# Keys and squares of an mLSTM head shared out anew between ScalarE and VectorE

## The chip, the cores and the metric

The program runs on one core of a Trainium2 chip. The metric is device time in microseconds for one execution, the median of several. The engines are called here as in the profile: PE is TensorE (PEld its weight loads), DVE is VectorE, ACT is ScalarE, POOL is GpSimd, SP is SyncE.

## The reference, cut to what matters

The reference is a transformer block followed by a second one, for 1024 positions and 1024 features, all in fp32. The change touches only the mLSTM of the first block: 4 heads of dimension 128, each run forward and backward in time, the two results added, normalised by their root mean square and gated:

```python
def step(carry, chunk):
    C, n, m = carry
    qc, kc, vc, ic, fc = chunk
    ...
    a = g[..., None] - b + ic
    m_new = jnp.maximum(g + m, jnp.max(a, axis=-1))
    decay = jnp.exp(g + m - m_new)
    w = jnp.exp(a - m_new[..., None])
    C = decay[..., None, None] * C + jnp.einsum('bhs,bhsv,bhsd->bhvd', w, vc, kc)
    n = decay[..., None] * n + jnp.einsum('bhs,bhsd->bhd', w, kc)
    return (C, n, m_new), h
...
h = (h_fw + h_bw).transpose(0, 2, 1, 3)
h = h * lax.rsqrt(jnp.mean(h * h, axis=-1, keepdims=True) + EPS)
h = h * norm_g.astype(jnp.float32).reshape(MLSTM_HEADS, MLSTM_HEAD_DIM)
h = h.reshape(B, S, MLSTM_WIDTH) * jax.nn.sigmoid(o_pre.astype(jnp.float32))
```

The keys weighted by `w` are needed once for each direction, since `w` differs. The mean of the squares is taken over the 128 numbers of a head, for each of the 1024 positions.

## The kernel before

All orders are fixed when the program is built. A plan (`schedule`) lists steps such as `("mk", h, u)`; each engine walks the same list and issues its own part of each step, in order, and counting semaphores tie the engines together. So an instruction that waits holds up everything behind it on its engine.

A head's 1024 positions lie as 8 chunks of 128. For the mLSTM the steps are, with `h` the head, `d` the direction and `u` a half of the positions:

- `mk` (PE `m_keys` L1072, DVE `m_keys` L1864): PE transposes 4 chunks of keys into one PSUM bank. DVE reads the bank twice, multiplies by the key coefficients of direction 0 and then of direction 1 and writes `kp[h % 2][0]` and `kp[h % 2][1]` (the rows call both `m_kp`, 128x512 each). Semaphore `k_made` counts both.
- `mv` (ACT `m_values` L1450): the transposed values are copied by ACT to `m_v`.
- `mm` (ACT L1466): ACT makes four exponentials of 128x128 for the decay weights `m_w`. `ms`, `wt`: scores by PE, product by DVE.
- `mu` (PE L1116, DVE `m_states` L1889): PE makes the chunk updates from `m_v` and `m_kp`; DVE runs them through a chain of 7 states `m_cs` (L1897 and L1901).
- `mo` (PE L1133, L1136): the outputs of a head and direction, in banks 5 to 7, in three parts.
- `mf`, `mi`, `mg`: the denominator `m_den`. ACT takes absolute values and a logarithm (L1474, L1475, L1477), DVE the maximum (`m_largest` L1904), ACT the exponential (L1482); then ACT (L1492, direction 0) or DVE (L1915, direction 1) scales the eight chunks into `m_hs`.
- `mq`, `mr`, `mn`: the normalisation. ACT squares all of `m_hs` in one instruction (L1499), DVE adds up the squares of each position (`m_sums`, L1920), ACT makes the inverse roots (L1503, L1505), DVE scales `m_hs` (`m_norm` L1922).
- `mtr` (PE L1143, DVE L1930): `m_hs` is turned back and gated.

The functions that transpose into or multiply into PSUM banks take them from a ring (`M_BANK`): two banks while the attention of the block still runs, five afterwards. `ring_emptied` (L865) gives what must be over before PE may write a bank again; for a bank that held keys this is that `kp` has been made from it.

Head 0 is prepared in the middle of the attention's last two heads, between its score and value steps. After the attention, `memory` (L235) writes out head `h` while it prepares head `h + 1`. In its order, shortened, an iteration is: `mo(h,0)` with `mk(h+1)` and `mv(h+1)` between its parts, `mf(h,0)`, `mm(h+1,0,0)`, `mi`, `mg`, `mu(h,1)`, `mm(h+1,0,1)`, `mtr(h-1)`, `mu(h+1,0)`, `mm(h+1,1)`, `ms`, `wt`, `mo(h,1)` with `mw(h+1)`, `mf(h,1)`, `mi`, `mg`, `mq(h)`, `mr(h)`, `mn(h)`. The iteration for head 3 prepares nothing, and the first products of the output projection come behind it.

Of the kernel before, what the change touches and what calls it, by code (L numbers as in the profile page):

```python
# [15 lines left out]
P = 128  # L16
# [49 lines left out]
for _name, _n in (("b_ada", 48), ("b_ada_2", 24), ("norm_mix_g", 8), ("norm_ffn_g", 8),  # L66
# [21 lines left out]
    "sel_in g_act g_vec g_tr g_cols st_hi st_lo sel_made sums_one k_tr k_made v_tr v_made m_mm e_made s_mm wgt wr_mm qp_made "  # L88
    "u_mm state out_mm den_abs den_ln den_max den_inv h_part h_sum o_sq o_sum o_ln o_r o_n o_tr o_done "

# [6 lines left out]
class Plan:  # L97
# [12 lines left out]
    def no(self, kind, *which):  # L110
        return self.number[(kind, *which)]
# [422 lines left out]
def tile_of(k):  # L534
    return slice(k * P, (k + 1) * P)


def build(nc, a, out):
# [3 lines left out]
    with ExitStack() as ctx:  # L542
# [322 lines left out]
        def ring_emptied(step):  # L865

            same = [x for x in M_RING[:M_RING.index(step)] if M_BANK[x] == M_BANK[step]]
            if not same:
                return None
            x = same[-1]  # L870
            if x[0] == "mk":
                return s["k_made"], 2 * no(*x)
            if x[0] == "mu":
                return s["state"], state_no(*x[1:])
            if x[0] == "ms":
                return s["wgt"], no("wt", x[1], 1, x[2])
            return s[{"mv": "v_made", "mm": "e_made", "mw": "qp_made", "mtr": "o_done"}[x[0]]], no(*x)
# [30 lines left out]
        def tensor(e):  # L908
# [158 lines left out]
            def ring(step):  # L1067
                if emptied := ring_emptied(step):
                    e.wait_ge(*emptied)
                return M_BANK[step]  # L1070

# [37 lines left out]
            def m_states(h, d, g):  # L1109
                bank = ring(("mu", h, d, g))  # L1110
                e.wait_ge(s["k_made"], 2 * no("mk", h, 1))
                e.wait_ge(s["v_made"], no("mv", h, 1))
                e.wait_ge(s["sums_one"], 1 + h % 2)
                for i, c in enumerate(M_GROUPS[g][:1 if g == 2 else 3]):
                    j = chunk(d, c)
                    x = e.matmul(ps[:, bank, m_piece(g, i)], kp[h % 2][d][:, j, :], v1[h % 2][:, j, :], start=True, stop=True, skip_group_check=True)  # L1116
                x.then_inc(s["u_mm"], 1)
# [145 lines left out]
        def scalar(e):  # L1263
# [150 lines left out]
            def gate(part):  # L1414
# [31 lines left out]
                elif part == 18:  # L1446
                    e.wait_ge(s["g_tr"], 4)
                    copy(dec_cols[:, :, :].rearrange("p a b -> p (a b)"), ps[:, aux_bank("gate", 18), 0:64]).then_inc(s["g_cols"], 1)

            def m_values(h, u):  # L1450
                e.wait_ge(s["v_tr"], no("mv", h, u))
                if h >= 2:
                    e.wait_ge(s["out_mm"], outs_no(2 * (h - 1)))
                copy(v1[h % 2][:, 4 * u:4 * u + 4, 0:P], ps[:, M_BANK[("mv", h, u)], :].rearrange("p (a b) -> p a b", a=4)).then_inc(s["v_made"], 1)
# [40 lines left out]
            def m_squares(h):  # L1495
                e.wait_ge(s["h_sum"], KT * (h + 1))
                if h:
                    e.wait_ge(s["o_sum"], h)
                e.activation(sq_m[:, :, :], hs[h % 2][:, :, :], ACT.Square).then_inc(s["o_sq"], 1)  # L1499

# [137 lines left out]
            def y_norm(n):  # L1638
# [3 lines left out]
                    "rsq": head_squares, "rln": head_roots, "attend": attend, "khi": k_high, "qhi": q_high, "mrow": mrow, "sc": scores, "take": take,  # L1642
                    "gate": gate, "mv": m_values, "mm": m_decays, "mf": m_finish, "mi": m_inverse, "mg": m_divide, "mq": m_squares,
                    "mr": m_roots, "mixk": mix, "wout": wout, "nr": norm, "nt": normed,
# [8 lines left out]
        def vector(e):  # L1653
            def tt(dst, x, z, op):
                return e.tensor_tensor(dst, x, z, op)  # L1655
# [208 lines left out]
            def m_keys(h, u):  # L1864
                e.wait_ge(s["k_tr"], no("mk", h, u))
                if h >= 2:
                    e.wait_ge(s["u_mm"], 6 * (h - 1))
                elif h == 1:
                    e.wait_ge(s["div"], 16)
                for d in range(2):  # L1870
                    x = kc_cols[:, 4 * u:4 * u + 4, d, h:h + 1].to_broadcast([P, 4, P])
                    tt(kp[h % 2][d][:, 4 * u:4 * u + 4, :], ps[:, M_BANK[("mk", h, u)], :].rearrange("p (a b) -> p a b", a=4), x,
                       ALU.mult).then_inc(s["k_made"], 1)

# [33 lines left out]
            def m_divide(h, d):  # L1908
                if d:
                    e.wait_ge(s["den_inv"], m_no(h, d) + 1)  # L1910
                    for c in range(KT):
                        j = chunk(1, c)
                        if c == 0:
                            e.wait_ge(s["h_part"], KT * (h + 1))
                        e.scalar_tensor_tensor(hs[h % 2][:, j, :], ps[:, 5 + c // 3, m_piece(c // 3, c % 3)][:, 0:P], den[1][:, c:c + 1],  # L1915
                                               hs[h % 2][:, j, :], ALU.mult, ALU.add).then_inc(s["h_sum"], 1)

            def m_sums(h):
                e.wait_ge(s["o_sq"], h + 1)
                e.tensor_reduce(o_sum[:, :], sq_m[:, :, :], AX_X, ALU.add).then_inc(s["o_sum"], 1)  # L1920

# [171 lines left out]
            def y_tile(n, k):  # L2093
# [9 lines left out]
                    "max": max_unit, "mrow": mrow, "div": divide, "gate": gate,  # L2103
                    "mk": m_keys, "wt": m_weights, "mw": m_queries, "mu": m_states, "mf": m_largest, "mg": m_divide, "mq": m_sums,
                    "mn": m_norm, "mtr": m_turn, "mixk": mix, "acc1": first_sums, "wout": wout, "nt": normed, "nl": normed_last, "fs": second_sum, "ft": final_normed,
# [310 lines left out]
```

## Time and profile before

| | us |
|---|---|
| median of 3 runs | 2150.54 (2149.56 to 2150.75) |
| the profiled execution, its own time | 2150.5 |
| its span in the profile | 2148.7 |
| PE busy in the span | 2043.8 (95%) |
| DVE, ACT busy | 1109.3, 871.1 |

The span is measured from the first to the last recorded instruction; what lies around it makes up the other 1.8 us. The mLSTM's steps lie between 491 and 650 us from the start of the span. In a row of the timeline there stand: start in us, length in us, engine, line, operation, what it writes and reads, how many instructions were merged, and in brackets how long the engine had been idle before and what ended the idle time. The length of a merged row reaches from the first start to the last end; the next instruction on ACT or DVE often starts a tenth of a microsecond before the end of the one ahead.

### The profile page before, as it was taken

The page shows a single profiled execution, that of the slowest core. Times are in us where ns is not written, and L with a number is a line of the kernel's source. Part 1 is how long each engine was busy: PE and PEld are TensorE (multiplying, and loading weights), DVE is VectorE, ACT ScalarE, POOL GpSimd, SP SyncE. Part 2 cuts the span into 40 slices and gives each one's busy share as a digit, 9 for nine tenths or more (in the row PEclk, how much of TensorE's full clock was granted, in tenths as well). Part 3 has the DMA queues.
Part 4 walks back from the last instruction along what each step waited for, and adds up shares of the span by engine and source line. Part 5 has one row for each costly group of instructions (what it writes and reads, how often), then busy time and mean ns, then how long its engine had stood idle before and what let it go on. Part 6 is the DMA issues. An engine that isn't in the chain of part 4 may idle for free.

```text
span 2148.7 us, 23710 instructions
## 1 busy us (share of the span) xinstructions
PE 2043.8 (95%) x9232; PEld 1590.5 (74%) x9232; DVE 1109.3 (52%) x1534; ACT 871.1 (41%) x1315; POOL 61.5 (3%) x115
## 2 busy tenths in 40 slices
PE   4999999999889899999999999999999999999797
PEld 1778876656777788888888888887787876776485
DVE  5785747555665655533354333437343454435535
ACT  4433345555443433233243232324424664445542
POOL 1001000000000000000000000000010000000000
PEclk9999999999999999999999999999999999999898
DMA  8335410000204546523333223334331010003043
GB/s 334 98 120 195 162 33 10 18 32 1 89 1 147 185 150 193 182 95 126 122 104 133 94 97 103 128 122 147 98 120 48 30 40 30 20 21 128 0 167 118
DMA packets 63198, 217.12 MB, mean 101 GB/s; under 512 B 6640, under 2 KB 7792, under 8 KB 62832
## 3 DMA queue, kind: packets, MB, share of 16 engines
q1 hardware_dynamic: 48944, 161.07, 22.2%
q0 software_dynamic: 14144, 54.53, 7.4%
q8 instruction: 75, 1.23, 0.2%
q14 instruction: 35, 0.29, 0.0%
HBM read 187.79 MB, written 25.17 MB: 99 GB/s over the span
## 4 chain that ended last, share of the span: by engine, by line
PE 84%; DVE 6%; ACT 4%; DMA 2%; issue 2%; SPq 1%; POOL 0%; DVEq 0%; ACTq 0%
PE ps L911 21%; PE ps L913 20%; PE ps L912 20%; PE ps L1045 8%; PE ps L1021 2%; PE ps L1022 2%; PE ps L988 2%; DMA w_raw<-in_weights 2%; PE ps L1003 1%; DMA cmask<-in_consts 1%; DVE slot L1655 1%; SPq L2206 1%; DVE w_lo L1659 1%; ACT w_hi L1265 1%; PE ps L991 1%
## 5 line engine op out<-in xcount | busy, mean ns | idle before, releaser
L911 PE MATMUL ps<-h_hi,w_hi 128*128 128x512 f32 x1504 | 600.0, 399 | 22.6 <-DVE h_lo L1692 11.0
L913 PE MATMUL ps<-h_hi,w_lo 128*128 128x512 f32 x1504 | 589.7, 392 | 0.0
L912 PE MATMUL ps<-h_lo,w_hi 128*128 128x512 f32 x1504 | 589.1, 392 | 0.0
L1659 DVE TENSOR_TENSOR w_lo<-w_raw,w_hi 128x1024 fp32r<-128x1024 f32 x222 | 271.8, 1225 | 496.5 <-ACT w_hi L1265 495.0
L1265 ACT ACTIVATE w_hi<-w_raw 128x1024 fp32r<-128x1024 f32 x222 | 234.7, 1057 | 527.2 <-DMA w_raw<-in_weights 525.5
L911 PEld LDWEIGHTS ps<-h_hi,w_hi 128*128 128x128 f32 x1504 | 285.2, 190 | 87.7 <-issue 21.7
L913 PEld LDWEIGHTS ps<-h_hi,w_lo 128*128 128x128 f32 x1504 | 284.2, 189 | 60.6
L912 PEld LDWEIGHTS ps<-h_lo,w_hi 128*128 128x128 f32 x1504 | 284.9, 189 | 59.0 <-issue 1.9
L1783 DVE TENSOR_REDUCE mh<-ps 128x1 f32<-128x512 f32 x192 | 124.8, 654 | 149.8 <-PE ps L988 70.7
L911 PE MATMUL ps<-hid_hi,w_hi 128*128 128x512 f32 x352 | 136.9, 389 | 0.0
L912 PE MATMUL ps<-hid_lo,w_hi 128*128 128x512 f32 x352 | 136.9, 389 | 0.0
L913 PE MATMUL ps<-hid_hi,w_lo 128*128 128x512 f32 x352 | 136.9, 389 | 0.0
L1045 PE MATMUL ps<-full_pf,full_v 128*128 128x512 f32 x256 | 132.0, 598 | 0.3 <-ACT full_pf L1402 0.2
L1045 PE MATMUL ps<-second_pf,second_v 128*128 128x128 f32 (+3 forms) x336 | 115.9, 447 | 7.5 <-ACT second_pf L1402 7.2
L1402 ACT ACTIVATE full_pf<-ps 128x512 f32<-128x512 f32 x128 | 76.2, 596 | 99.5 <-PE ps L1022 99.0
L911 PE MATMUL ps<-mix_hi,w_hi 128*128 128x512 f32 x256 | 103.2, 403 | 6.9 <-DVE mix_lo L1659 6.9
L912 PE MATMUL ps<-mix_lo,w_hi 128*128 128x512 f32 x256 | 101.5, 397 | 0.0
L913 PE MATMUL ps<-mix_hi,w_lo 128*128 128x512 f32 x256 | 101.2, 395 | 0.0
L1402 ACT ACTIVATE second_pf<-ps,cum_cols 128x512 f32<-128x512 f32 (+1 forms) x96 | 55.4, 579 | 111.3 <-PE ps L1026 75.4
L1021 PE MATMUL ps<-full_qq,full_kk 128*128 128x512 f32 x128 | 91.0, 711 | 0.1
L1021 PE MATMUL ps<-second_qq,second_kk 128*128 128x128 f32 (+3 forms) x168 | 85.3, 508 | 0.3 <-issue 0.3
L911 PEld LDWEIGHTS ps<-hid_hi,w_hi 128*128 128x128 f32 x352 | 66.1, 188 | 13.8
(302 smaller groups left out, 2593.5 us busy)
## 6 DMA issues: line engine op xcount, KB each, us to landing
w_raw<-in_weights SPq DMA_DIRECT2D x222, 512.0 KB, 3.5
ada_next<-in_ada POOLq DMA_DIRECT2D x32, 512.0 KB, 4.7
ada_last<-in_ada POOLq DMA_DIRECT2D x24, 512.0 KB, 4.3
ada_first<-in_ada SPq DMA_DIRECT2D x8, 1024.0 KB, 14.9
m_scratch<-y POOLq DMA_DIRECT2D x12, 512.0 KB, 4.8
xt<-in_x SPq DMA_DIRECT2D x2, 2048.0 KB, 16.9
y<-m_scratch SPq DMA_DIRECT2D x4, 1024.0 KB, 5.9
x_again<-in_x SPq DMA_DIRECT2D x16, 256.0 KB, 3.7
```

The source lines that it names most:

```text
L911: e.matmul(o, w_hi[slot][:, tile_of(kw)], hi, start=start, stop=False)
L912: e.matmul(o, w_hi[slot][:, tile_of(kw)], lo, start=False, stop=False)
L913: return e.matmul(o, w_lo[slot][:, tile_of(kw)], hi, start=False, stop=stop)
L988: x = e.matmul(ps[:, bank, 0:k1 - k0], q(qt), A.kk[kb][:, k0:k1], start=True, stop=(kind == "full"), skip_group_check=True)
L991: x = e.matmul(ps[:, bank, 0:k1 - k0], sel_f[:, h, :], cum_split[:, k0:k1], start=False, stop=not diagonal, skip_group_check=True)
L1021: e.matmul(o, A.kk[kb][:, keys], A.qq[b][:, q], start=True, stop=False, skip_group_check=True)
L1022: x = e.matmul(o, A.ka[kb][0:65, keys], A.qa[b][0:65, q], start=False, stop=not masked, skip_group_check=True)
L1045: x = e.matmul(o, A.v[kb][:, kt, :], A.pf[p3][:, c:c + q1 - q0], start=(u == 0 and kind != "band"), stop=False, skip_group_check=True)
L1265: return e.activation(dst, src, ACT.Copy)
L1402: e.activation(A.pf[p3][:, c0:c1], ps[:, bank, c0:c1], ACT.Exp, scale=SC, **bias).then_inc(s["p_exp"], 1)
L1659: return e.tensor_tensor(dst, src, hi.bitcast(F32), ALU.subtract)
L1783: x = e.tensor_reduce(to, ps[:, bank, 0:k1 - k0], AX_X, ALU.max)
```

## The change

Three things change, all in the mLSTM.

The squares: instead of one ACT instruction of 128x1024 and a DVE reduction, ACT issues eight instructions of 128x128, each of which also writes the sum of its squares to a column of `o_sum` (an accumulator output). They wait, as before, for all eight chunks of `m_hs`. The step `m_sums` of DVE and the semaphore `o_sq` are gone.

The keys: DVE makes only the keys of direction 0. Those of direction 1 are made by ACT, with four instructions of 128x128 for each half, which wait until DVE's have been made (`k_made`), and count `k_late`. In ACT's order they stand where `mk` stands in the plan, ahead of the copies of the values `mv`.

The waits of PE: a bank that held keys is free when both `k_made` and `k_late` have come; the updates `mu` wait for the one of their direction.

```diff
     def ring_emptied(step):
             if x[0] == "mk":
-                return s["k_made"], 2 * no(*x)
+                return s["k_made"], no(*x)
...
             def ring(step):
                 if emptied := ring_emptied(step):
                     e.wait_ge(*emptied)
+                    if emptied[0] is s["k_made"]:
+                        e.wait_ge(s["k_late"], emptied[1])
...
             def m_states(h, d, g):
                 bank = ring(("mu", h, d, g))
-                e.wait_ge(s["k_made"], 2 * no("mk", h, 1))
+                e.wait_ge(s["k_late" if d else "k_made"], no("mk", h, 1))
...
         def scalar(e):
+            def m_keys(h, u):
+
+                e.wait_ge(s["k_made"], no("mk", h, u))
+                if h >= 2:
+                    e.wait_ge(s["u_mm"], 6 * (h - 1))
+                elif h == 1:
+                    e.wait_ge(s["div"], 16)
+                else:
+                    e.wait_ge(s["g_cols"], 4)
+                for c in range(4):
+                    x = e.activation(kp[h % 2][1][:, 4 * u + c, :], ps[:, M_BANK[("mk", h, u)], tile_of(c)], ACT.Copy,
+                                     scale=kc_cols[:, 4 * u + c, 1, h:h + 1])
+                x.then_inc(s["k_late"], 1)
...
             def m_squares(h):
                 e.wait_ge(s["h_sum"], KT * (h + 1))
                 if h:
-                    e.wait_ge(s["o_sum"], h)
-                e.activation(sq_m[:, :, :], hs[h % 2][:, :, :], ACT.Square).then_inc(s["o_sq"], 1)
+                    e.wait_ge(s["o_r"], h)
+                for c in range(KT):
+                    x = e.activation(sq_m[:, c, :], hs[h % 2][:, c, :], ACT.Square, accum_out=o_sum[:, c:c + 1])
+                x.then_inc(s["o_sum"], 1)
...
         def vector(e):
             def m_keys(h, u):
-                for d in range(2):
-                    x = kc_cols[:, 4 * u:4 * u + 4, d, h:h + 1].to_broadcast([P, 4, P])
-                    tt(kp[h % 2][d][:, 4 * u:4 * u + 4, :], ps[:, M_BANK[("mk", h, u)], :].rearrange("p (a b) -> p a b", a=4), x,
-                       ALU.mult).then_inc(s["k_made"], 1)
+                x = kc_cols[:, 4 * u:4 * u + 4, 0, h:h + 1].to_broadcast([P, 4, P])
+                tt(kp[h % 2][0][:, 4 * u:4 * u + 4, :], ps[:, M_BANK[("mk", h, u)], :].rearrange("p (a b) -> p a b", a=4), x,
+                   ALU.mult).then_inc(s["k_made"], 1)
...
-            def m_sums(h):
-                e.wait_ge(s["o_sq"], h + 1)
-                e.tensor_reduce(o_sum[:, :], sq_m[:, :, :], AX_X, ALU.add).then_inc(s["o_sum"], 1)
```

PE's instructions stand in the same order as before; only their waits differ. The order on ACT and DVE changes as follows.

ACT between the end of head 0 and the denominator of head 1, before (`m_hs_192` is head 0's, `m_v_179` holds the values of head 2, `m_den_185` is the denominator of direction 0):

```order
L1499 ACTIVATE m_sq<-m_hs_192 128x1024
L1503 ACTIVATE o_root<-o_sum,small 128x8
L1505 ACTIVATE o_root<-o_root 128x8
L1265 ACTIVATE m_v_179<-ps 128x4x128 x2
L1474 ACTIVATE m_den_185<-ps 128x6
L1475 ACTIVATE m_den_185<-ps 128x2
L1477 ACTIVATE m_den_185<-m_den_185,small 128x8
```

and the same place now:

```order
L1516 ACTIVATE m_sq,o_sum<-m_hs_192 128x128 x8
L1521 ACTIVATE o_root<-o_sum,small 128x8
L1523 ACTIVATE o_root<-o_root 128x8
L1462 ACTIVATE m_kp_181<-ps,kc_cols 128x128 x8
L1267 ACTIVATE m_v_179<-ps 128x4x128 x2
L1490 ACTIVATE m_den_185<-ps 128x6
L1491 ACTIVATE m_den_185<-ps 128x2
L1493 ACTIVATE m_den_185<-m_den_185,small 128x8
```

Eight scalings of keys stand between the roots and the copies of the values, and the denominator of head 1 comes behind both.

DVE at the same place, before (`m_kp_180` and `m_kp_181` are the keys of head 2 for direction 0 and 1, `m_cs_177` the states of head 1, direction 1):

```order
L1920 TENSOR_REDUCE o_sum<-m_sq 128x8
L1655 TENSOR_TENSOR m_hs_192<-m_hs_192,o_root 128x1024
L1655 TENSOR_TENSOR m_kp_180<-ps,kc_cols 128x512
L1655 TENSOR_TENSOR m_kp_181<-ps,kc_cols 128x512
L1655 TENSOR_TENSOR m_kp_180<-ps,kc_cols 128x512
L1655 TENSOR_TENSOR m_kp_181<-ps,kc_cols 128x512
L1655 TENSOR_TENSOR m_den_185<-m_den_185,n_cols 128x8
L1897 COPY m_cs_177<-ps 128x129
L1901 SCALAR_TENSOR_TENSOR m_cs_177<-m_cs_177,dec_cols,ps 128x129 x6
```

and now:

```order
L1673 TENSOR_TENSOR m_hs_192<-m_hs_192,o_root 128x1024
L1673 TENSOR_TENSOR m_kp_180<-ps,kc_cols 128x512 x2
L1673 TENSOR_TENSOR m_den_185<-m_den_185,n_cols 128x8
L1914 COPY m_cs_177<-ps 128x129
L1918 SCALAR_TENSOR_TENSOR m_cs_177<-m_cs_177,dec_cols,ps 128x129 x6
L1943 SCALAR_TENSOR_TENSOR y<-ps,small,y 128x512 x2
```

Three instructions are gone from DVE's row. The maximum of the denominator (`m_den_185<-m_den_185,n_cols`) still stands ahead of the states, and its input now comes from behind ACT's scalings.

ACT in the attention, where head 0 is prepared, before:

```order
L1402 ACTIVATE full_pf_126<-ps 128x512
L1381 ACTIVATE full_qa_121<-ps 1x512
L1402 ACTIVATE full_pf_127<-ps 128x512
L1265 ACTIVATE full_qq_117<-y 64x512
L1265 ACTIVATE m_v_179<-ps 128x4x128
```

and now:

```order
L1404 ACTIVATE full_pf_126<-ps 128x512
L1383 ACTIVATE full_qa_121<-ps 1x512
L1462 ACTIVATE m_kp_181<-ps,kc_cols 128x128 x4
L1404 ACTIVATE full_pf_127<-ps 128x512
L1267 ACTIVATE full_qq_117<-y 64x512
L1267 ACTIVATE m_v_179<-ps 128x4x128
```

Four scalings stand between two exponentials of the attention (`full_pf`), ahead of the copy of the values; the four for head 0's first half stand in the same way one exponential earlier.

## Rows read from the trace of the kernel before

**Rows 1.** The page, part 1: busy time and share of the span.

```profile
PE 2043.8 (95%) x9232; PEld 1590.5 (74%) x9232; DVE 1109.3 (52%) x1534; ACT 871.1 (41%) x1315; POOL 61.5 (3%) x115
```

**Rows 2.** Windows: stretch, its length, then busy us of each engine, PE clock, DMA.

```profile
484.00:540.00 56.00, 54.38 (x233) 34.63 (x232) 30.58 (x57) 28.92 (x59) 0.00 (x0) 1.00 0.00 1
564.00:585.00 21.00, 19.76 (x152) 18.32 (x152) 17.45 (x38) 10.24 (x36) 0.00 (x0) 0.92 0.00 1
```

**Rows 3.** Groups by form, 544 to 650: busy us, mean ns | idle before.

```profile
L1492 ACT ACTIVATE m_hs<-ps,m_den 128x128 f32<-128x128 f32 x32 | 8.7, 383 | 0.1
L1655 DVE TENSOR_TENSOR m_kp<-ps,kc_cols 128x512 f32<-128x512 f32 x12 | 7.4, 682 | 1.9 <-PE ps L1078 1.9
L1499 ACT ACTIVATE m_sq<-m_hs 128x1024 f32<-128x1024 f32 x4 | 4.2, 1057 | 9.0 <-DVE m_hs L1915 9.0
L1920 DVE TENSOR_REDUCE o_sum<-m_sq 128x8 f32<-128x1024 f32 x4 | 4.9, 1220 | 3.4 <-ACT m_sq L1499 3.4
```

**Rows 4.** Groups by form, 690 to 900: VectorE reading its accumulator.

```profile
L1677 DVE DVE_READ_ACCUMULATOR2_ANT mod<- 128x1 f32 x20 | 1.6, 82 | 0.0
```

**Rows 5.** Timeline where head 0 is prepared, DVE, ACT and PE's weight loads.

```profile
496.19 1.29 DVE L1655 TENSOR_TENSOR m_kp<-ps,kc_cols 128x512 f32<-128x512 f32 x2 [0.60 <-PE ps L1078]
...
496.66 0.60 ACT L1402 ACTIVATE full_pf<-ps 128x512 f32<-128x512 f32 x1 [1.41 <-PE ps L1022]
...
498.19 0.60 ACT L1265 ACTIVATE m_v<-ps 128x512 f32<-128x512 f32 x1 [0.28 <-PE ps L1084]
...
500.58 0.60 ACT L1265 ACTIVATE m_v<-ps 128x512 f32<-128x512 f32 x1
...
501.41 0.78 PEld L1116 LDWEIGHTS ps<-m_v,m_kp 128*128 128x128 f32 x6 [0.53 <-ACT m_v L1265]
```

**Rows 6.** Timeline of head 0's iteration, DVE, ACT and PE.

```profile
547.01 2.48 DVE L1655 TENSOR_TENSOR m_kp<-ps,kc_cols 128x512 f32<-128x512 f32 x4 [1.91 <-PE ps L1078]
...
550.55 0.18 ACT L1474 ACTIVATE m_den<-ps 128x6 f32<-128x6 f32 x1 [0.25 <-PE ps L1136]
...
555.55 0.50 PE L1091 MATMUL ps<-nm_stack,sel 128*128 128x512 f32 x1 [1.94 <-ACT m_w L1466]
```

**Rows 7.** Timeline of head 1's iteration, ACT.

```profile
565.69 1.06 ACT L1499 ACTIVATE m_sq<-m_hs 128x1024 f32<-128x1024 f32 x1 [2.23 <-DVE m_hs L1915]
568.03 0.30 ACT L1503 ACTIVATE o_root<-o_sum,small 128x8 f32<-128x8 f32 x1 [1.29 <-DVE o_sum L1920]
...
570.11 1.09 ACT L1265 ACTIVATE m_v<-ps 128x512 f32<-128x512 f32 x2 [1.54 <-PE ps L1084]
571.44 0.18 ACT L1474 ACTIVATE m_den<-ps 128x6 f32<-128x6 f32 x1 [0.24 <-PE ps L1136]
...
571.71 0.30 ACT L1477 ACTIVATE m_den<-m_den,small 128x8 f32<-128x8 f32 x1
```

**Rows 8.** Timeline of head 1's iteration, DVE.

```profile
568.61 1.23 DVE L1655 TENSOR_TENSOR m_hs<-m_hs,o_root 128x1024 f32<-128x1024 f32 x1 [0.61 <-ACT o_root L1505]
569.75 2.48 DVE L1655 TENSOR_TENSOR m_kp<-ps,kc_cols 128x512 f32<-128x512 f32 x4
572.14 0.16 DVE L1655 TENSOR_TENSOR m_den<-m_den,n_cols 128x8 f32<-128x8 f32 x1
572.64 0.29 DVE L1897 COPY m_cs<-ps 128x129 f32<-128x129 f32 x1 [0.33 <-PE ps L1116]
```

**Rows 9.** Timeline of head 2's iteration, DVE.

```profile
597.07 1.57 DVE L1901 SCALAR_TENSOR_TENSOR m_cs<-m_cs,dec_cols,ps 128x129 f32<-128x129 f32 x4 [0.70 <-PE ps L1116]
598.97 1.41 DVE L1930 SCALAR_TENSOR_TENSOR y<-ps,small,y 128x512 f32<-128x512 f32 x2 [0.33 <-PE ps L1143]
```

**Rows 10.** Timeline of PE: heads 1 and 2 on keys, and head 3's iteration.

```profile
566.73 1.57 PE L1078 MATMUL ps<-ident,y 128*128 128x128 f32 x8
...
587.60 1.04 PE L1078 MATMUL ps<-ident,y 128*128 128x128 f32 x8
...
615.63 0.63 PE L1143 MATMUL ps<-ident,m_hs 128*128 128x128 f32 x4 [0.38 <-DVE m_hs L1655]
```

More of the change, by code:

```diff
@@ L88 @@
     "sel_in g_act g_vec g_tr g_cols st_hi st_lo sel_made sums_one k_tr k_made v_tr v_made m_mm e_made s_mm wgt wr_mm qp_made "
-    "u_mm state out_mm den_abs den_ln den_max den_inv h_part h_sum o_sq o_sum o_ln o_r o_n o_tr o_done "
+    "u_mm state out_mm den_abs den_ln den_max den_inv h_part h_sum k_late o_sum o_ln o_r o_n o_tr o_done "
     "mix_hi mix_lo xa_in0 xa_in1 x1_made x1_kept silu gmul hid_hi hid_lo xc_in0 xc_in1 x2_made xb_kept "
@@ L1642, in scalar @@
                     "rsq": head_squares, "rln": head_roots, "attend": attend, "khi": k_high, "qhi": q_high, "mrow": mrow, "sc": scores, "take": take,
-                    "gate": gate, "mv": m_values, "mm": m_decays, "mf": m_finish, "mi": m_inverse, "mg": m_divide, "mq": m_squares,
+                    "gate": gate, "mk": m_keys, "mv": m_values, "mm": m_decays, "mf": m_finish, "mi": m_inverse, "mg": m_divide, "mq": m_squares,
                     "mr": m_roots, "mixk": mix, "wout": wout, "nr": norm, "nt": normed,
@@ L2103, in vector @@
                     "max": max_unit, "mrow": mrow, "div": divide, "gate": gate,
-                    "mk": m_keys, "wt": m_weights, "mw": m_queries, "mu": m_states, "mf": m_largest, "mg": m_divide, "mq": m_sums,
+                    "mk": m_keys, "wt": m_weights, "mw": m_queries, "mu": m_states, "mf": m_largest, "mg": m_divide,
                     "mn": m_norm, "mtr": m_turn, "mixk": mix, "acc1": first_sums, "wout": wout, "nt": normed, "nl": normed_last, "fs": second_sum, "ft": final_normed,
```

## The prediction

> **What bounds the kernel now.** First the page's busy times: PE is busy for 2043.8 of 2148.7 us, the others about half or less [rows 1]. A microsecond on DVE or ACT is therefore worth something only where PE waits for it, and the change touches nothing outside the mLSTM. Next the windows over that stage. While head 0 is prepared, in the attention, PE is busy for 54.38 of 56 us. In the iteration of head 1 it is busy for 19.76 of 21, and its granted clock there averages 0.92; DVE has 17.45 [rows 2]. Then the timeline, engine by engine. What the reader is to see in it is who waits for whom between one head and the next: ACT squares the head, DVE adds up, ACT makes the roots, DVE scales the head and then the next keys, and runs the states [rows 7, 8]. From 568.61 DVE has hardly a gap, so in head 1 DVE sets the pace. ACT meanwhile copies the values and stands ready early: it begins head 1's denominator at 571.44 [rows 7], and DVE's maximum follows at 572.14 [rows 8].
>
> **The squares.** Before, from the start of the squares to the start of the logarithm is 568.03 - 565.69 = 2.34 us: 1.06 on ACT, 1.22 on DVE and two hand-overs [rows 3, 7]. Now ACT issues eight instructions with an accumulator output. They wait for all eight chunks of the head as before, so nothing starts sooner. No row shows ACT with an accumulator. Call the new time from squares to logarithm X. From below: if cutting up and accumulating cost nothing, X is the 1.1 us of the one instruction [rows 3]. From above: each chunk takes the full 0.38 us of a 128x128 activation with no overlap, and a read of the accumulator as long as the smallest ACT instruction, 0.18 [rows 3, 7]: 8 x 0.56 = 4.5. Nearer rows: eight 128x128 activations one behind the other take 2.17 (0.27 each); with 0.08 for a read, as DVE's own read of its accumulator has it [rows 4], that is 0.35, or 0.46 if the read lets nothing overlap. The middle is 0.40 a chunk, X = 3.2, a loss of 0.86 against 2.34. The 2.17 is the length of the eight scalings by L1492, 32 in all at 383 ns each in 8.7 us busy [rows 3].
>
> On this the Trainium skill, page "ScalarE: Activation LUTs", section "What ACT_TABLE_LOAD costs", states 186 ns plus 0.833 ns per element for an ACTIVATE with immediate operands, and 93 ns of overlap back to back: 200 ns a chunk, 1.7 us for eight by an estimate from that page. The trace agrees for the large form (1057 ns for 1024 elements) and shows nothing of the accumulator. With 1.7 the sum below would be 2.5.
>
> **The keys.** DVE loses one 682 ns multiplication for each half of the keys, 0.62 from start to start (2.48 for four) [rows 3, 8]. ACT gains four scalings for each, the same form as L1492: PSUM in, a column as scale. That is 2.17 for a head's eight. The same page of the Trainium skill, section "Rules for kernel authors", says to use VectorE rather than ScalarE for a multiplication. The rows agree in fp32 too, 682 ns against half of 2.17. Who is slower matters less, though, than where the eight stand: behind DVE's, and ahead of ACT's copies of the values and of the denominator, for whose maximum DVE waits in order ahead of its states. PE's two new waits fall behind these and cost nothing by themselves.
>
> *Head 0, in the attention.* DVE's first multiplication of the second half ends at 496.19 + 0.68 = 496.87. ACT scales from 496.9 and has room for the next instruction at 498.0, so the exponential that stood at 496.66 is 1.34 late. The copy waited 0.28 for PE at 498.19 [rows 5], so 1.06 remains, and ACT is full from there to the last copy at 500.58. PE's update at 501.41 was released by that copy: it comes 1.06 late. PE is the bound here, so 1.1 stays.
>
> *Head 0's iteration* (keys of head 1). ACT used to wait here. Now: DVE's multiplication from 547.01, 0.68 and 0.04 to hand over, eight scalings 2.17, two copies 1.09 [rows 6, 7] gives 550.99 for the denominator that began at 550.55. ACT's chain from there ends in the decay weights for which PE waited at 555.55 [rows 6]. PE is late by 0.4. DVE's gain of 1.24 is hidden: it had nothing to do.
>
> *Head 1's iteration* (keys of head 2), from the squares at 565.69 [rows 7, 8]: X 3.2; logarithm to DVE's scaling of the head 0.58; 1.14 to the keys; 0.68 + 0.04 to ACT; 2.17 of scalings; 1.09 of copies; from the denominator's start to its maximum 572.01 - 571.44 and a hand-over, 0.60. Sum 9.50, so the maximum at 575.2 instead of 572.14, the states at 575.4 instead of 572.64. Here DVE turns from busy to idle, for 4.58 - 1.30 = 3.3 us (0.72 + 2.17 + 1.09 + 0.60, less two multiplications). The states, the turned head and the next states follow in one row, and PE's outputs behind them: 2.7 late.
>
> *Head 2's iteration* is the same sum with one rounding of weights more on both engines. The maximum is 3.0 late; DVE had waited 0.70 and 0.33 for PE behind it [rows 9], which absorb 1.0. So 2.0.
>
> *Head 3's iteration* has no keys. PE waited for the scaled head at 615.63 [rows 10]: late by X - 2.34 = 0.86. The last head's squares lie beside the output projection, which starts without them. With 0.86 more they still do, cost 0.
>
> **Sum.** 1.1 + 0.4 + 2.7 + 2.0 + 0.9 = 7.1 us. The profiled execution took 2150.5 (span 2148.7 and 1.8 around it), the median of the runs shown is 2150.54, so both give 2157.6. X enters three times: 2.2 gives 2154.6, 4.5 gives 2161.5, and 1.1 gives 2151.3.
>
> **Rivals.**
> - *The accumulator is nearly free* (X from 1.1 to 2.2). For it: the two fixed costs seen are small, 0.08 and 0.18. Against: a result that is read out must be complete first. 0.8 to 4.1 late, at 2.0 it is 3.5: 2154.0. By the page's 200 ns a chunk it would be here. Within 0.2%.
> - *PE's clock falls in the new gaps.* The eight transposes of head 1 took 1.57 where head 2's took 1.04 [rows 10], and the granted clock of that window is 0.92, a mix of 2.4 and 1.2 GHz: 0.08 of 21 us [rows 2] is 1.7 us of full clock lost in one spell. In heads 1 and 2 PE now idles for longer, in pieces. Two spells on the path: 3.4 more, 2161.0. Against: after 1.94 us of idle at 555.55 a 128x512 product took 0.50 [rows 6], so not every such gap brings a spell.
> - *The accumulator is dear* (X near 4.5): 2161.5.
> - *DVE's shorter queue decides* and the time falls. The mechanism: DVE is the pace from 568.61 on, and loses 1.24 in heads 1 and 2; if squares cost the bare 1.1, another 1.24 in three places. 2 x 1.24 + 3 x 1.24 = 6.2 less, 2144.3. It decides only if ACT has the logarithm of the denominator ready when DVE has finished its two multiplications, 1.30 after their start. By my sum it is ready 0.72 + 2.17 + 1.09 + 0.60 = 4.58 after it, 3.3 too late whatever X is. Unlikely.
>
> **How the numbers follow.** The forecast as summed, 4.3 to 9 us late, 48%; accumulator free 21%; clock 15%; accumulator dear 10%; DVE decides 6%. 0.2% of the time is 4.3 us, about what a measurement of this kernel can tell from no change. Faster by more than that: the last case, 5%. Within it: the free accumulator and what little the last case leaves, 22%. Slower: 73%. Predicted 2157.6; the range reaches down into the free accumulator and up over clock and dear accumulator: 2152 to 2163.
>
> **What the profile would show.** The squares: eight ACT instructions of 128x128 and the logarithm 3.2 behind the first; below 2.2 or above 4 one of the accumulator's rivals holds. The keys: DVE idle for some 3 us ahead of the head's denominator in heads 1 and 2, with ACT busy on `m_kp` and `m_v`; if DVE goes on without a gap, the main step is wrong. Attention: the update of head 0 waits 1.6 for ACT's copy instead of 0.5. Clock: the granted clock of the windows of heads 1 and 2, by the lengths of equal groups of PE. I would be wrong throughout if the stretch from the first keys to the output projection grew by less than 4 us.

## The result, and the profile after

| | before | after |
|---|---|---|
| median of 12 runs each, us | 2149.59 | 2155.72 |
| lowest, highest | 2146.83, 2152.56 | 2152.10, 2160.15 |
| profiled execution's span | 2148.7 | 2154.1 |

The ratio is 1.0028, with an interval of 1.0019 to 1.0036: 4.1 to 7.7 us slower, 6.1 by the medians. Forecast were 7.1 slower and 2157.6.

The page of the profile after, part 1, against [rows 1]: DVE has lost 9.3 us and 12 instructions, ACT has gained 13.8 and 92, and PE has the same work.

```profile
PE 2043.8 (95%) x9232; PEld 1590.2 (74%) x9232; DVE 1100.0 (51%) x1522; ACT 884.9 (41%) x1407; POOL 61.5 (3%) x115
```

ACT of the profile after, from the squares of head 0 to the logarithm of head 1's denominator:

```profile
565.16 0.31 ACT L1516 ACTIVATE m_sq<-m_hs 128x128 f32<-128x128 f32 x1 [2.22 <-DVE m_hs L1932]
565.38 0.19 ACT L1516 ACTIVATION_READ_ACCUMULATOR m_sq<-m_hs 128x1 f32 x1
565.47 0.29 ACT L1516 ACTIVATE m_sq<-m_hs 128x128 f32<-128x128 f32 x1
...
567.64 0.30 ACT L1521 ACTIVATE o_root<-o_sum,small 128x8 f32<-128x8 f32 x1
567.97 0.21 ACT L1523 ACTIVATE o_root<-o_root 128x8 f32<-128x8 f32 x1
570.08 2.17 ACT L1462 ACTIVATE m_kp<-ps,kc_cols 128x128 f32<-128x128 f32 x8 [1.89 <-DVE m_kp L1673]
572.09 1.13 ACT L1267 ACTIVATE m_v<-ps 128x512 f32<-128x512 f32 x2
573.04 0.25 ACT L1490 ACTIVATE m_den<-ps 128x6 f32<-128x6 f32 x1
```

and DVE of the same stretch:

```profile
568.21 1.23 DVE L1673 TENSOR_TENSOR m_hs<-m_hs,o_root 128x1024 f32<-128x1024 f32 x1 [3.09 <-ACT o_root L1523]
569.36 1.28 DVE L1673 TENSOR_TENSOR m_kp<-ps,kc_cols 128x512 f32<-128x512 f32 x2
573.71 0.17 DVE L1673 TENSOR_TENSOR m_den<-m_den,n_cols 128x8 f32<-128x8 f32 x1 [3.07 <-ACT m_den L1493]
573.80 0.29 DVE L1914 COPY m_cs<-ps 128x129 f32<-128x129 f32 x1
```

Two things are to be seen. The squares hardly cost: from the first of them to the logarithm there are 567.64 - 565.16 = 2.48 us against 2.34. And DVE, which ran without a gap at this place in [rows 8], now stands idle for 3.07 us ahead of the maximum, while ACT first waits for DVE's keys (1.89), then scales, copies and takes the denominator. From the start of the squares to the maximum 8.55 us pass, before 6.45.

### The profile page after: what moved, and what is told of

Its sections match the earlier page's. It is cut to its first block, busy times and chain, and to the rows that moved or that the text cites. A ratio compares the mean times of both kernels' runs of the same rounds, so it can differ in the third digit from the quotient of the medians.

```text
span 2154.1 us, 23801 instructions
## 1 busy us (share of the span) xinstructions
PE 2043.8 (95%) x9232; PEld 1590.2 (74%) x9232; DVE 1100.0 (51%) x1522; ACT 884.9 (41%) x1407; POOL 61.5 (3%) x115
## 4 chain that ended last, share of the span: by engine, by line
PE 83%; DVE 6%; ACT 5%; DMA 3%; issue 2%; SPq 1%; POOL 0%; DVEq 0%; ACTq 0%
PE ps L911 20%; PE ps L913 20%; PE ps L912 20%; PE ps L1045 8%; PE ps L1021 2%; PE ps L1022 2%; PE ps L988 2%; DMA w_raw<-in_weights 2%; PE ps L1003 1%; DMA cmask<-in_consts 1%; SPq L2219 1%; DVE slot L1673 1%; DVE w_lo L1677 1%; ACT w_hi L1267 1%; PE ps L991 1%
## 5 line engine op out<-in xcount | busy, mean ns | idle before, releaser
L1045 PEld LDWEIGHTS ps<-second_pf,second_v 128*128 128x128 f32 x336 | 60.2, 198 | 24.4 <-ACT second_pf L1404 10.7
```

Source lines behind the costliest of these rows:

```text
L1045: x = e.matmul(o, A.v[kb][:, kt, :], A.pf[p3][:, c:c + q1 - q0], start=(u == 0 and kind != "band"), stop=False, skip_group_check=True)
```

## The experiments

The time of a run is the median of 5 to 12 executions, and its ratio is to the kernel before on the same chip. The kernel before had medians of 2148.6 to 2150.8 on the chips used, so two runs are best compared by what each is over it; the changed kernel is 6.1 over it. `e12_before_again` is a single execution.

**Which part of the change costs?** `e1_squares` is the kernel before with the new `m_squares` alone. `e2_keys` is the changed kernel with the old squares and `m_sums`:

```diff
 e1:            keys as before; in m_squares
-                e.activation(sq_m[:, :, :], hs[h % 2][:, :, :], ACT.Square)
+                for c in range(KT):
+                    x = e.activation(sq_m[:, c, :], hs[h % 2][:, c, :], ACT.Square, accum_out=o_sum[:, c:c + 1])
 e2:            keys as changed; this edit taken back, m_sums again on DVE
```

> Only the squares are changed: eight with an accumulator output on ScalarE, VectorE's reduction gone, both directions of the keys on VectorE as before. Theory A (the keys' place in ScalarE's row costs the time): from squares to logarithm 2.48 us in place of 2.34, so 0.14 for each of heads 0, 1 and 2, in all 0.4 us over the kernel before: 2150.0, no measurable difference. Theory B (the split squares cost the time): most of the 6.1 us, 2154 or more. Theory C (half of it arises after the mLSTM stage, whatever the stage does): the piece in the stage is 0.4, the whole is 2 or more.

Measured: 2150.53 against 2150.47, ratio 1.0005 (0.9996 to 1.0013). Split squares cost nothing that can be measured.

> Only the keys are changed: direction 1 on ScalarE behind VectorE's, squares in one instruction with VectorE's reduction as before. Theory A: VectorE idles some 3 us ahead of the maximum in heads 1 and 2 as in the changed kernel, the stage up to the output projection is 3.4 us longer than before (0.4 in the attention, 0.2, 1.7, 1.1), time 2153 to 2155. Theory B: below 2150.6. Theory C: 3.4 in the stage and 2 more behind it, 2155.

Measured: 2155.75, ratio 1.0028 (1.0017 to 1.0038), the changed kernel's own ratio. The whole loss is the keys'. Theory B is refuted.

**Is it where the scalings stand in ACT's row?** `e3_keys_later`: in the iterations that prepare heads 1 to 3 ACT scales behind the copies of the values and the denominator.

```diff
             def m_finish(h, d):
+                m_denominator(h, d)
+                if d == 0 and h < 3:
+                    for u in range(2):
+                        m_keys_late(h + 1, u)
```

> The changed kernel with one thing moved: for heads 1 to 3 ScalarE's eight scalings of keys stand behind the denominator of direction 0 and the copies of the values instead of ahead of both. Theory A: VectorE's 3.07 us of idle ahead of the maximum in heads 1 and 2 fall below 0.5; the states then wait at most for TensorE's updates, which wait for the scalings, and each of heads 1 and 2 is 1.2 to 1.8 shorter: 2.4 to 3.6 less than the changed kernel, 2152 to 2153.5. If the load on ScalarE and not its place is the cause: within 0.5 us of the changed kernel, 2155.7.

Measured: 2157.98, ratio 1.0041 (1.0027 to 1.0055), no gain at all. DVE, ACT and PE of this kernel in head 1's iteration:

```profile
572.70 1.28 DVE L1682 TENSOR_TENSOR m_kp<-ps,kc_cols 128x512 f32<-128x512 f32 x2
574.74 2.15 ACT L1465 ACTIVATE m_kp<-ps,kc_cols 128x128 f32<-128x128 f32 x8
574.87 0.17 DVE L1682 TENSOR_TENSOR m_den<-m_den,n_cols 128x8 f32<-128x8 f32 x1 [0.89 <-ACT m_den L1502]
...
575.96 2.16 PE L1118 MATMUL ps<-m_v,m_kp 128*128 128x129 f32 x14 [1.26 <-issue]
576.90 0.29 DVE L1923 COPY m_cs<-ps 128x129 f32<-128x129 f32 x1 [1.87 <-PE ps L1118]
```

The idle time ahead of the maximum fell from 3.07 to 0.89 us (forecast: below 0.5), but the states behind it now wait 1.87 for PE. PE's updates start 1.2 behind ACT's first scalings. The row names no releaser; by the code PE needs the bank of the keys' first half, which is free only when its four scalings have been made (the wait that `ring` gained). So the scalings lie on the path by two ways, ACT's row and PE's bank. In head 1's iteration moving them back on one only uncovers the other: from squares to squares it took 23.70 us, in the two profiles of the changed kernel 23.82 and 23.81. In head 2's it did gain (23.71 against 24.95), but in head 0's iteration PE's first decay row came 12.45 behind its first output, where it had come 10.6 behind it, and that outweighed the gain. This corrected theory A: what counts is when the scalings end.

**Can they end earlier?** `e7_scalar_keys_first`: for heads 1 to 3 ACT scales first and DVE behind it.

```diff
 scalar:
-                e.wait_ge(s["k_made"], no("mk", h, u))
+                e.wait_ge(s["k_tr" if h else "k_made"], no("mk", h, u))
 vector:
-                e.wait_ge(s["k_tr"], no("mk", h, u))
+                e.wait_ge(s["k_late" if h else "k_tr"], no("mk", h, u))
```

> The changed kernel, but in heads 1 to 3 ScalarE scales the second direction's keys of a half first, as soon as TensorE has turned them, and VectorE scales the first direction's behind it. Theory A (the loss is ScalarE's row, which starts only when VectorE's first scaling is done, so that the eight scalings end 2 us later than need be, ahead of the denominator that VectorE waits for): the row starts at the end of the reciprocal roots (568.2 and not 570.1), the maximum of head 1 comes 1.5 to 2 us earlier than in the changed kernel, that of head 2 the same, and the time is 3 to 4.5 us under the changed kernel's, 2151 to 2153. Theory E (the loss is the sum of work on ScalarE, whatever its place): the maximum stays within 0.5 us, 2155 to 2156.5. Theory F (VectorE now waits for ScalarE, and the first direction's states are late by as much): 2155 or more, with TensorE waiting over 2.5 us for VectorE's keys in head 1.

Measured: 2152.02, ratio 1.0004 (0.9995 to 1.0012). ACT and then DVE of this kernel, head 1's iteration:

```profile
570.49 0.21 ACT L1523 ACTIVATE o_root<-o_root 128x8 f32<-128x8 f32 x1
570.60 2.15 ACT L1462 ACTIVATE m_kp<-ps,kc_cols 128x128 f32<-128x128 f32 x8
...
574.22 0.17 DVE L1673 TENSOR_TENSOR m_den<-m_den,n_cols 128x8 f32<-128x8 f32 x1 [0.74 <-ACT m_den L1493]
```

The scalings follow the roots with no wait, the maximum comes 574.22 - 567.68 = 6.54 us behind the squares (changed 8.55, before 6.45), and the loss is gone within what can be measured: 1.2 us over the kernel before, where on the same chip the changed kernel was 6.9 over it (`e9_changed_again`, below). The 1.89 that ACT waited for DVE was the costly part of theory A; theories E and F are refuted.

**Would earlier squares pay?** Squares can start on a chunk as soon as DVE has finished it. `e5_squares_by_chunk` does this on the changed kernel, `e6_chunk_squares_alone` on `e1_squares`, `e8_keys_first_chunk_squares` on `e7_scalar_keys_first`.

```diff
             def m_squares(h):
-                e.wait_ge(s["h_sum"], KT * (h + 1))
...
                 for c in range(KT):
-                    x = e.activation(sq_m[:, c, :], hs[h % 2][:, c, :], ...)
+                    j = chunk(1, c)
+                    e.wait_ge(s["h_sum"], KT * h + c + 1)
+                    x = e.activation(sq_m[:, j, :], hs[h % 2][:, j, :], ...)
```

> The changed kernel, but each of the eight squares waits only for its own chunk of the head, in the order in which VectorE makes them. Theory A: the squares run beside VectorE's 2.16 us; from its last chunk to the logarithm it is 0.6 us in place of 2.48, and everything behind comes 1.9 earlier in heads 0, 1 and 2: 5.6 less than the changed kernel, 2150. If the squares are not on the path (theory that ScalarE's keys alone set the pace): no change, 2155.7.

Measured: 2151.86, ratio 1.0007 (0.9999 to 1.0016): 3.9 us under the changed kernel's 2155.72. It is 1.4 over the kernel before on its chip where the changed kernel was 6.1 over it, a gain of 4.7; 5.6 was expected. DVE and ACT of this kernel, head 0's end:

```profile
564.41 2.16 DVE L1933 SCALAR_TENSOR_TENSOR m_hs<-ps,m_den,m_hs 128x128 f32<-128x128 f32 x8 [0.28 <-ACT m_den L1498]
564.79 0.31 ACT L1517 ACTIVATE m_sq<-m_hs 128x128 f32<-128x128 f32 x1 [0.42 <-DVE m_hs L1933]
...
567.27 0.30 ACT L1522 ACTIVATE o_root<-o_sum,small 128x8 f32<-128x8 f32 x1
```

The squares run beside DVE's row, and the logarithm comes 0.70 us behind its end at 566.57, where it came 2.5 behind it in the changed kernel.

> The kernel before, its keys all on VectorE, with each square waiting only for its own chunk of the head and accumulating its sum. Theory A (the squares' start is on the path of every head; the keys are untouched): the squares split alone cost nothing, and the last square ends about 1.75 us earlier in a head, as the run with the keys on both engines showed (squares 564.79, logarithm 567.27). Three passages of that path (heads 0 to 2) and the last head: 4 to 6 us less than the kernel before, 2144.5 to 2146.5 us. In the trace DVE's idle time ahead of the denominator's maximum stays at 1.7. Theory D (earlier squares only uncover another wait, since the run on the changed kernel brought 3.9 where 5.6 were expected): under 2 us less, 2148.5 to 2150.5, and DVE or ACT waits as long elsewhere in the head.

Measured: 2146.67 against 2150.82, ratio 0.9980 (0.9971 to 0.9990). Theory D is refuted, and this kernel beats both. The idle time ahead of the scaling of the head in DVE's row is 1.28 here where it was 3.1 in `e1_squares`.

> Both edits at once: ScalarE's scalings first in heads 1 to 3, and each square as soon as its chunk is there. Theory A: the two gains add, 3 to 4.5 us for the place of the scalings and 3.9 for the squares, 7 to 8.5 under the changed kernel's 2155.7, so 2147 to 2149 us, which is under the kernel before. Theory E (ScalarE's load decides): only the squares' gain, 2151 to 2153.

Measured: 2148.46, ratio 0.9994 (0.9985 to 1.0002). The two gains add (7.3 under the changed kernel's 2155.72); against the kernel before itself the interval reaches past no change. It is 1.8 above `e6_chunk_squares_alone`, by medians whose intervals overlap; in both profiles the iteration of head 0 took 18.7 us and that of head 2 took 21.0 or 21.1. So even in the best order found, taking the keys from DVE brought nothing that can be seen.

**Do the rows' sum and the medians agree?** `e9_changed_again` and `e12_before_again` are second profiles of the two kernels.

> The changed kernel once more, for a second profile of it. Theory A (its loss comes from head 0 to head 2 of the mLSTM and what TensorE's clock does there differs from one execution to the next): 2155 to 2156.5 us; VectorE's idle time ahead of the maximum in heads 1 and 2 is 3.1 us again within 0.1, the granted clock of 540 to 660 us differs from 0.97, and the span differs by what that makes. Theory C (a systematic loss behind the mLSTM): from the last row of the output projection to the end the kernel takes again over 1 us longer than the kernel before did.

Measured: 2157.75, ratio 1.0035 (1.0023 to 1.0047). DVE's two idle times are 3.07 again, and the granted clock of 540 to 660 us is 0.91 (0.97 in the first profile).

> The kernel before once more, for a second profile of it. Theory A: the waits of the mLSTM are the same to 0.1 us (VectorE idle 1.7 ahead of head 1's maximum), and the granted clock of 540 to 660 us may differ from 0.93; from the last tile of the feed-forward's second product to the end of the program it scatters by over 1 us from the first profile's 674.6, as the kernels with the same code there do. Theory C (a systematic loss of the changed kernel behind the mLSTM): it is again within 1 us of 674.6.

Measured, one execution: 2148.64. The waits are those of before, but for the 0.33 us that DVE's states had waited for PE in [rows 8]. Head 1's iteration took 21.55 us from squares to squares, and 21.96 in the first profile. Windows of that iteration, first the second profile of before, then the second of the changed kernel (the clock is the third number from the end):

```profile
564.00:585.00 21.00, 17.83 (x149) 16.22 (x149) 17.49 (x39) 10.49 (x37) 0.00 (x0) 1.00 0.00 1
```

```profile
564.00:585.00 21.00, 17.48 (x134) 15.84 (x133) 13.29 (x34) 13.77 (x60) 0.00 (x0) 0.92 0.00 1
```

In the first pair the clocks were the other way round, 0.92 before [rows 2] and 1.00 after. So one pair of profiles doesn't price the clock; it differs between executions of one kernel.

The profiles do show where the time goes. From DVE's first keys to PE's first product of the output projection:

| | first keys to output projection, us | from there to the end, us |
|---|---|---|
| before, two profiles | 130.8, 130.4 | 1525.4, 1525.5 |
| `e1_squares` | 130.8 | 1528.2 |
| `e6_chunk_squares_alone` | 129.0 | 1525.1 |
| changed, two profiles | 134.6, 136.8 | 1528.1, 1526.4 |
| `e2_keys` | 136.6 | 1525.9 |
| `e7_scalar_keys_first` | 132.7 | 1529.3 |

Behind it the four profiles with all keys on DVE average 1526.1 us and the ten with some keys on ACT 1525.8. By the landmark of the expectation, which lies 22.6 us behind PE's last product of the feed-forward in all of these profiles, those four took 674.6, 674.4, 678.3 and 675.7, the changed kernel 678.1 and 677.0. The second profile of before was within 1 us of the first, as theory C wanted, but `e1_squares`, with the same code there, wasn't. So the loss that the profiles show lies in the mLSTM, 3.8 us in the first pair and 6.4 in the second; a systematic one behind it is not shown, and one of a microsecond isn't excluded either.

**Which head pays?** `e10_head_0_alone` and `e13_head_0_again` (the same kernel) give ACT the scalings of head 0 only, `e11_heads_1_to_3_alone` the others:

```diff
 scalar, m_keys:
+                if not (h == 0):
+                    return
 vector, m_keys:
+                for d in range(1 if h == 0 else 2):
```

> The changed kernel, with ScalarE scaling the second direction's keys of head 0 alone (those in the attention's last part); in heads 1 to 3 VectorE scales both directions, as before. Theory A (each head pays by its own rows): the attention's last part is 0.4 us longer, the iteration of head 0 costs 0.2 and the squares 0.14 a head, together about 1 us: 2150.5 to 2152. Theory G (VectorE's shorter row in the attention lets TensorE run ahead and wait, so that its clock falls, and that is what the medians show beyond the rows' sum of 3.8): 2152.5 to 2154.

Measured: 2154.83 against 2148.58, ratio 1.0032 (1.0019 to 1.0044), six executions, the profiled one far below the other five.

> The complement: ScalarE scales the second direction's keys of heads 1 to 3, and head 0 is as in the kernel before. Theory A: the maxima of heads 1 to 3 are as late as in the changed kernel (VectorE idle 3.07 us ahead of each), and nearly the whole loss is here, 4.5 to 6 us: 2155 to 2157. Theory G: 2152.5 to 2154.

Measured: 2155.98, ratio 1.0040 (1.0027 to 1.0052). Theory A had 2155 to 2157. But the two parts together would be 13.6 us, more than twice the whole change, so at least one of the medians misleads.

> ScalarE's scalings in head 0 alone, once more, since its median (2154.8, six runs from 2145.9 to 2155.3) stood 6.2 us over the kernel before where the path's rows leave about 1, and its profiled run was the fastest of the six. Theory A (the rows' sum is the cost): this median is 1 to 2.5 us over the kernel before, the six runs were a chance. Theory G (head 0's part alone brings the loss, by TensorE's clock in the mLSTM): 4 us or more over the kernel before, and a profile of a typical run shows a passage at a lower clock that the kernel before does not have, most likely in head 0's iteration, which then takes 22.2 us from TensorE's first output to the squares where both profiles of before took 20.55. Theory H (all edits at once and head 0 alone cost the same because the loss lies behind the mLSTM): the stretch from the last tile of the second product to the end is longer than 677 us.

Measured: 2152.57 against 2149.32, ratio 1.0015 (1.0006 to 1.0025): 3.3, between the theories' figures. PE of this kernel in head 0's iteration:

```profile
554.48 0.50 PE L1093 MATMUL ps<-nm_stack,sel 128*128 128x512 f32 x1 [1.95 <-ACT m_w L1483]
...
555.05 2.88 PE L1103 MATMUL ps<-y 128*128 128x128 f32 x16
```

and of the second profile of before:

```profile
553.96 0.50 PE L1091 MATMUL ps<-nm_stack,sel 128*128 128x512 f32 x1 [1.96 <-ACT m_w L1466]
...
554.54 2.00 PE L1101 MATMUL ps<-y 128*128 128x128 f32 x16
```

Both had waited as long, 1.95 and 1.96 us, and then the same sixteen products took 2.88 in the one and 2.00 in the other. Such a spell at the lower clock comes and goes between executions of one kernel too: in the two profiles of the changed kernel this wait was 2.15 and 2.14 us, and only the second had a spell behind it. The windows of 556 to 566 us, in the same order:

```profile
556.00:566.00 10.00, 7.99 (x53) 7.63 (x52) 7.27 (x17) 1.24 (x6) 0.00 (x0) 0.83 0.01 3
```

```profile
556.00:566.00 10.00, 7.99 (x67) 7.62 (x67) 7.87 (x18) 1.80 (x5) 0.00 (x0) 1.00 0.01 2
```

The iteration took 22.16 from PE's first output to the squares where both profiles of before took 20.5: 1.6 us, theory G's mark. By all the profiles (from PE's first output of head 0 to DVE's scaling of direction 1): the four with DVE making all keys took 18.34 to 18.36; of the ten with any of them on ACT two took 18.34 and 18.54 (the first profile of the changed kernel is one), seven 19.98 to 20.19, and `e3_keys_later`, where PE also waits longer, 22.01. Were the spell equally likely in both, none in four beside eight in ten would come about once in 67 draws (15 of 1001).

That shared keys bring this spell is not shown, though. The stretch was chosen after the profiles had been seen, and in three of the eight (`e7_scalar_keys_first`, `e10_head_0_alone`, `e11_heads_1_to_3_alone`) the spell came at another wait, PE's 2.06 us ahead of its first output, which the kernel before has as well. PE of `e11_heads_1_to_3_alone`, where no key has been made by ACT up to then:

```profile
542.95 0.71 PE L1135 MATMUL ps<-m_v,m_w 128*128 128x129 f32 x4 [2.06 <-DVE y L1674]
...
544.16 1.68 PE L1080 MATMUL ps<-ident,y 128*128 128x128 f32 x8
```

and of the second profile of before:

```profile
543.55 0.71 PE L1133 MATMUL ps<-m_v,m_w 128*128 128x129 f32 x4 [2.06 <-DVE y L1655]
...
544.77 1.04 PE L1078 MATMUL ps<-ident,y 128*128 128x128 f32 x8
```

Nor is the first spell the only one: the second profile of the changed kernel has more of them in the iterations of heads 1 to 3. What the profiles show is what a spell costs in this stretch, 1.6. Theory H stays open: the stretch behind was over its mark of 677 here (678.1), but 670.3 in `e10_head_0_alone`, the same kernel, and 678.3 in `e1_squares`, whose keys are DVE's.

## Why the prediction was right

The side, the mechanism and its place were right; that the number came so close is in part luck, as two errors nearly made up for each other, terms too large and a clock left out. The terms, from landmarks of the two pairs of profiles:

| term | forecast | first pair | second pair |
|---|---|---|---|
| attention, first keys to PE's first output of head 0 | 1.1 | 52.98 - 52.62 = 0.36 | 0.37 |
| head 0's iteration, PE's first output to squares | 0.4 | 20.73 - 20.54 = 0.19 | 22.37 - 20.55 = 1.82 |
| head 1, squares to squares | 2.7 | 23.82 - 21.96 = 1.86 | 23.81 - 21.55 = 2.26 |
| head 2, squares to squares | 2.0 | 24.94 - 23.69 = 1.25 | 1.25 |
| head 3, squares to the output projection | 0.9 | 12.14 - 12.01 = 0.13 | 0.71 |
| sum | 7.1 | 3.8 | 6.4 |

The pairs differ by where PE's clock fell. In the second the changed kernel has a spell in head 0's iteration (1.63 more) and one in head 3's (0.58 more); in the first it was the kernel before that had one, in head 1's (0.41). Without these the change costs 0.36 + 0.19 + 2.26 + 1.25 + 0.13 = 4.2 us on the path.

The forecast had said that it would be wrong throughout if this stretch grew by less than 4 us. In the first pair it grew by 3.8, so by its own sign it failed there, and in the second by 6.4. The sign was too sharp for one pair of executions. What speaks for the mechanism is DVE's idle time of 3.07, which stands in both profiles of the changed kernel, and `e7_scalar_keys_first`.

*The squares.* The term was over-sized: X is 2.48, not 3.2, so it costs 0.14 and not 0.86 in each of three places; that is 2.2 of the 2.9 by which 7.1 is over 4.2, and most of the rest is the attention's. A chunk follows the last by 0.29 us where 0.40 was taken. The rival "accumulator nearly free" was right in its mechanism, though X lies in the forecast's stretch above 2.2; `e1_squares` bears out that the split costs nothing that can be measured. The Trainium skill's 200 ns a chunk (page "ScalarE: Activation LUTs", section "What ACT_TABLE_LOAD costs") gives 1.7 for the eight, by the prediction's estimate from that page; the trace has 0.29 a chunk, 0.09 more. (With 1.7 the sum would have been 2.6, where the prediction has 2.5.)

*The keys in heads 1 and 2.* The chain was as forecast: with the squares at 2.48, the sum says 8.78 from the squares to the maximum, measured are 8.55. The rest is that rows which follow one another start 0.1 ahead of the end of the last: eight scalings take 2.01 and two copies 0.95 from start to start, not 2.17 and 1.09. The same takes head 0's 0.4 down towards its 0.19. DVE's idle time, forecast 3.3, is 3.07. What absorbs the delay behind it was right in kind for head 2: 1.25 of the 2.1 stay. In head 1 all of it stays.

*Attention.* Forecast 1.1, measured 0.36. This step failed. It counted what ACT adds, and not what DVE's shorter row gives back: DVE makes the attention's maximum `mx` right behind its keys. DVE and PE of the profile before:

```profile
493.73 0.15 DVE L1655 TENSOR_TENSOR mx<-mh 128x4 f32<-128x4 f32 x1
494.03 0.60 PE L1003 MATMUL ps<-ident,mx 128*1 128x128 f32 x4 [1.07 <-DVE mx L1655]
```

DVE, ACT and PE's weight loads of the profile after:

```profile
491.45 0.69 DVE L1673 TENSOR_TENSOR m_kp<-ps,kc_cols 128x512 f32<-128x512 f32 x1 [0.60 <-PE ps L1080]
492.06 0.15 DVE L1673 TENSOR_TENSOR mx<-mh 128x4 f32<-128x4 f32 x1
...
495.24 1.14 ACT L1462 ACTIVATE m_kp<-ps,kc_cols 128x128 f32<-128x128 f32 x4 [0.83 <-DVE m_kp L1673]
...
499.93 0.60 ACT L1267 ACTIVATE m_v<-ps 128x512 f32<-128x512 f32 x1
500.75 0.75 PEld L1118 LDWEIGHTS ps<-m_v,m_kp 128*128 128x128 f32 x6 [1.27 <-ACT m_v L1267]
```

The maximum comes 0.6 behind the keys, where it came 1.2 behind them (its start is 493.73, the keys' 492.53), and PE, which had waited for it, goes on that much sooner. PE's later wait for ACT's copy is 1.27; forecast were 1.6, and [rows 5] has 0.53.

*The clock.* The forecast gave it no term, and the runs point to it for the rest of the measured 6.1. The mean granted clock of the whole program was 0.9833, 0.9831 and 0.9837 for the kernel before on three chips, and 0.9816, 0.9814 and 0.9816 for `e2_keys`, `e9_changed_again` and `e11_heads_1_to_3_alone` beside it; the twelve executions of the changed kernel that gave 2155.72 have 0.9823. Over 191 executions of all kernels, the deviation of a time from its kernel's mean goes with the deviation of its clock by 1.13 us for each 0.001 (correlation -0.73). 0.0017 to 0.0021 are then 1.9 to 2.4 us, and the 0.0010 of the twelve (against 0.9833) 1.1; with the 4.2 of the path this makes 5.3 to 6.6. That is an account from many runs, not an experiment on the clock: a lower clock goes with more idle time of PE, and part may be counted twice. The rival "PE's clock falls in the new gaps" thus held beside the forecast's mechanism, but not by its price, nor in the heads that it named. Its price of 1.7 was read from [rows 2]; that same spell, in head 1 of the kernel before, cost 0.41 on the path (21.96 against 21.55). In head 1 of the changed kernel one cost nothing (23.81 with it, 23.82 without), and in head 0 one cost 1.6. And spells stood behind gaps that the kernel before has too, not only behind longer ones.

*The rival on the other side*, that DVE's shorter queue decides, is out: ACT's logarithm was ready 4.3 us behind the start of DVE's two multiplications, forecast 4.58. A kernel faster than before was possible, but by the wait that the change left alone: the squares stood behind all eight chunks.

Open stays why head 0's part alone came out 6.2 us slower in one series: the profiles of both series have the mLSTM 2.5 to 2.9 longer than before, which is near the other's 3.3. Open, too, is why the changed kernel's mean clock is lower, and when a gap of some 2 us brings a spell.

## What to carry over

Ask for work that is moved to another engine when it ends, not only which engine has room: its end is waited for in the new engine's row and in the bank that it reads. If two engines read one bank in turn, let the one go first that is free first; on one chip this alone took the loss from 6.9 to 1.2 us. And look at what an instruction waits for before dividing it: eight squares behind one wait brought nothing, each behind its own chunk 4.2 us.

## What was not expected of the hardware

- A read of ACT's accumulator has a record of 187 ns (32 of them), yet the next square starts some 0.09 us behind the start of the read (565.38, 565.47): the squares follow each other every 0.29 us, with a read between.
- PE's clock after the same gap differs between executions of one kernel: behind a wait of 2.15 and 2.14 us in the two profiles of the changed kernel, head 0's iteration took 20.73 and 22.37. What such a spell costs depends on who else is waited for there: 1.6 us in head 0, 0.41 in head 1 of the kernel before, nothing in head 1 of the changed kernel.
- Medians of few executions mislead here: the same kernel was 6.2 us over the kernel before by 6 executions and 3.3 by 11.
